# Two dense heads scored together on groups of the array's rows, and the remainder of an expert's tokens turned back by one transpose

## The reference

```python
a = rms_norm(h, attn_norm_g)
q_s, k_s, v_s, q_lat, kv_lat, k_rope = split(a @ w_in)
y_a = windowed_gqa(...)        # 8 heads of 64, 2 key heads, keys within 128 tokens and the meta tokens, ALiBi, sink
y_b = latent_attention(...)    # 8 dense heads: q = rms_norm(...) is 64 columns (nope) and 32 rotated (rope),
                               # k likewise with one rope part for all heads; every query sees all 1040 keys
h = h + concat(y_a, y_b) @ w_out
m = rms_norm(h, ffn_norm_g)
logits = m @ router_w + router_b          # 32 experts, each token goes to 4
y = swiglu(m_e @ w_gate[e], m_e @ w_up[e]) @ w_down[e] + b_down[e]      # of the tokens m_e of expert e
h = h + sum of y, weighted by the gate
```

## Time and profile before

| | |
|---|---|
| time, median of 3 runs | 2257.07 us (2256.37 to 2257.84) |
| the profiled execution | 2257.38 us, its span 2255.3 us |
| PE busy | 2211.1 us, 98% |
| weight loads (PEld) | 1743.8 us, 77% |
| DVE busy | 815.5 us, 36% |
| ACT busy | 485.9 us, 22% |
| POOL busy | 205.5 us, 9% |
| transfers | 490.37 MB, mean 217 GB/s |

### The profile page before, as it was taken

One profiled execution on the slowest core, in us unless ns is written; L12 is line 12 of the kernel. 1 busy time (PEld: TensorE's weight loads), 2 busy tenths in 40 slices (PEclk: granted clock), 3 DMA queues, 4 the chain that ended last, 5 costly groups with the idle time before them and its releaser, 6 DMA issues.

```text
span 2255.3 us, 37720 instructions
## 1 busy us (share of the span) xinstructions
PE 2211.1 (98%) x15544; PEld 1743.8 (77%) x15544; DVE 815.5 (36%) x2465; ACT 485.9 (22%) x1235; POOL 205.5 (9%) x229
## 2 busy tenths in 40 slices
PE   8998999999999899999999999999999999999998
PEld 4554666666666877887899999998788878878876
DVE  4555655555556322222222222222222222222222
ACT  3343544544445000000111111110000000001000
POOL 1000000000001111111111111010000000000000
PEclk9999999999999899999999999999999999999999
DMA  4000500000005897878878888899998998999881
GB/s 164 29 1 2 170 11 29 31 29 29 24 16 195 262 313 244 280 262 280 301 266 308 294 320 302 293 320 326 328 343 310 327 343 310 330 340 325 314 307 20
DMA packets 208573, 490.37 MB, mean 217 GB/s; under 512 B 22395, under 2 KB 23867, under 8 KB 208224
## 3 DMA queue, kind: packets, MB, share of 16 engines
q1 hardware_dynamic: 191824, 448.71, 55.1%
q0 software_dynamic: 14960, 39.07, 6.9%
q10 hardware_dynamic: 1616, 0.14, 0.1%
HBM read 463.49 MB, written 28.88 MB: 218 GB/s over the span
## 4 chain that ended last, share of the span: by engine, by line
PE 66%; issue 0%; DMA 0%; POOL 0%; POOLq 0%; ACT 0%; DVE 0%
PE gu_bank L2107 43%; PE ya_bank L2168 13%; PE ya_bank L2140 6%; PE yb_bank L2181 1%; PE xa_bank L2077 1%; PE xb_bank L2085 0%; PE yb_bank L2125 0%; PE xa_bank L2124 0%; PE ya_bank L2157 0%; DMA x_rows<-ffn_rows,first_tab 0%; POOLq L1669 0%; POOL out_y L1822 0%; ACT y_rows L1887 0%; DVE y_rows L1978 0%; PE yb_bank L2195 0%
## 5 line engine op out<-in xcount | busy, mean ns | idle before, releaser
L2107 PE MATMUL gu_bank<-xT,ring_head 128*128 128x128 f32 (+10 forms) x4160 | 507.5, 282 | 0.8 <-issue 0.8
L2107 PEld LDWEIGHTS gu_bank<-xT,ring_head 128*128 128x128 f32 x4160 | 498.7, 191 | 7.6 <-issue 7.3
L2107 PE MATMUL gu_bank<-xT,ring 128*128 128x128 f32 (+8 forms) x4032 | 484.8, 280 | 0.0
L2107 PEld LDWEIGHTS gu_bank<-xT,ring 128*128 128x128 f32 x4032 | 477.0, 191 | 3.8 <-issue 3.6
L1932 DVE TENSOR_SCALAR g_in<-gu_bank,bias_cur 128x128 f32<-128x128 f32 (+10 forms) x256 | 91.9, 359 | 644.7 <-PE gu_bank L2107 644.3
L1877 ACT ACTIVATE sig<-g_in 128x128 f32<-128x128 f32 (+10 forms) x256 | 80.9, 316 | 815.8 <-DVE g_in L1932 815.8
L2168 PE MATMUL ya_bank<-ring,hidden 128*128 128x512 f32 x480 | 208.9, 593 | 0.0
L2168 PEld LDWEIGHTS ya_bank<-ring,hidden 128*128 128x128 f32 x480 | 90.0, 190 | 107.8 <-issue 105.0
L556 PE MATMUL proj_bank<-w_in_sb,normT 128*128 128x512 f32 (+3 forms) x384 | 128.2, 487 | 0.0
L1285 PE MATMUL score_bank<-ring_head 96*128 96x512 f32 x256 | 126.9, 620 | 0.0
L1978 DVE TENSOR_TENSOR y_rows<-ya_bank,b_row 128x512 f32<-128x512 f32 x46 | 29.7, 687 | 268.7 <-PE ya_bank L2168 257.3
(11 more groups left out here) (348 smaller groups left out, 2285.4 us busy)
## 6 DMA issues: line engine op xcount, KB each, us to landing
ring<-in_w_down SPq DMA_DIRECT2D x42, 2048.0 KB, 12.2
ring_head<-in_w_up SPq DMA_DIRECT2D x33, 2048.0 KB, 8.9
ring_head<-in_w_gate SPq DMA_DIRECT2D x32, 2048.0 KB, 14.1
ring<-in_w_gate SPq DMA_DIRECT2D x32, 2048.0 KB, 14.6
ring<-in_w_up SPq DMA_DIRECT2D x31, 2048.0 KB, 9.1
ring_head<-in_w_down SPq DMA_DIRECT2D x22, 2048.0 KB, 11.9
b_row<-in_b_down SPq DMA_DIRECT2D x32, 512.0 KB, 9.2
xt<-in_x SPq DMA_DIRECT2D x8, 512.0 KB, 3.9
```

What stands on the lines that cost most here:

```text
L2107: last = nc.tensor.matmul(gu_bank[:, f % 2, i * 256:i * 256 + width], w[:, k, c * P:(c + 1) * P], xT[:, k, 0:width], start=(k == 0), stop= ...
```

## The change

In attend a step now has two heads or two local pairs: four dense steps and two local ones a tile (`UNITS` is 6). The keys and queries of the dense heads are stored as two arrays each: the nope parts of two heads on the two 64-row halves, and the rope parts of two heads, each twice, on four groups of 32 rows, one for each half of the keys. A dense step's scores are four rope matmuls of 32 rows (L1355 of the new kernel), one to each of the four banks of `score_bank`, and four nope matmuls of 64 rows (L1360) that add to them. The next scores wait until DVE has read all four banks (`max_ready`, `band_ready`).

DVE reads each bank once, by the operation that local heads had: it adds a column of zeros, keeps a running maximum and writes the scores to `probs` (in odd steps to `late_probs`, a part of the ring's fourth piece). ACT's exponential works in place there. The values of a step are done in two parts, with the transposes of inverse sums, normed rows and logits between them. The meta scores are eight matmuls of two heads each in four groups of output columns, and one transpose instead of two. The out projection takes the dense half of its inner dimension first and waits for the local half (`swa_mixed`) later. The first expert's fourth weight piece waits for the last transposes of `late_probs`.

In project, a tile has six transposes of keys instead of eight, by pairs of heads, and eight of queries as before; two more gain constants are fetched.

In experts, ACT copies the first 128 columns of a tall chunk to `yT` and the others to a tile `yT_more` with 16 columns a chunk, and one transpose (L2191) turns all eight chunks' rests. They come out as one part of 128 columns per partition, so the bias and the gate and slot tables are fetched by eight small transfers each, and the sum is added by parts of rows, as in the wider turns.

The diff, cut to the matmuls and transposes, DVE's passes and the tall turns:

```diff
-                    for hf in range(2):
-                        transposes(t, f"kT{hf}", [(i, k_raw[0:n, 4 * hf + i, :]) for i in range(4)])
+                    transposes(t, "kT0", [(i, k_nope[0:n, 2 * i:2 * i + 2, :].rearrange("p h c -> p (h c)"))
+                                          for i in range(4)])
+                    transposes(t, "kT1", [(i, k_rope[0:n, i].rearrange("p b s c -> p (b s c)")) for i in range(2)])
                     if t < MT:
                         pe.wait_ge(q_ready, tiles_to(s + 1))
-                        for hf in range(2):
-                            transposes(t, f"qT{hf}", [(i, q_raw[:, 4 * hf + i, :]) for i in range(4)])
+                        transposes(t, "qT0", [(i, q_nope[:, 2 * i:2 * i + 2, :].rearrange("p h c -> p (h c)"))
+                                              for i in range(4)])
+                        transposes(t, "qT1", [(i, q_rope[:, 2 * i:2 * i + 2].rearrange("p h a c -> p (h a c)"))
...
+                def dense_max(n, b, half):
+                    t, i = divmod(n, UNITS)
+                    h = 2 * i + b
+                    if b == 0:
+                        if half:
+                            dve.wait_ge(scores_done, n + 1)
+                        else:
+                            dve.wait_ge(half_done, n + 1)
+                            dve.wait_ge(meta_read, t + 1)
+                    link(v.tensor_tensor_reduce(
+                        out=probs_of(n)[:, b, half * 512:(half + 1) * 512], in0=score_bank[:, 2 * b + half, :], in1=zeros[:].to_broadcast([P, 512]),
+                        scale=1.0, scalar=half_max[:, b:b + 1] if half else meta_max[:, t % 2, h:h + 1],
+                        op0=ALU.add, op1=ALU.max, accum_out=all_max[:, b:b + 1] if half else half_max[:, b:b + 1]))
+                    if half:
+                        v.tensor_scalar(neg_max[:, n % 2, b:b + 1], all_max[:, b:b + 1], -1.0, None, ALU.mult)\
+                            .then_inc(max_ready, 1)
...
+                def wait_read(n):
+                    t, i = divmod(n, UNITS)
+                    if i < DENSE:
+                        pe.wait_ge(max_ready, t * MLA_HEADS + 2 * i + 2)
+                    else:
+                        pe.wait_ge(band_ready, t * SWA_HEADS + 4 * (i - DENSE) + 4)
 
                 def scores(n):
                     t, i = divmod(n, UNITS)
-                    j = at_fill["unit", n]
-                    bank = score_bank[:, j % 2, :]
-                    wait_fill_free(pe, j)
-                    if i < MLA_HEADS:
+                    if n:
+                        wait_read(n - 1)
+                    if i == OUT + 1 and t >= 1:
+                        pe.wait_ge(attn_added, t)
+                    if i < DENSE:
+                        m, s = divmod(i, 2)
+                        for g in range(4):
+                            b, half = g // 2, g % 2 ^ s
+                            r = slice(g * ROPE, (g + 1) * ROPE)
+                            nc.tensor.matmul(score_bank[:, 2 * b + half, :], q_roT[r, i, cols(t)], k_roT[r, m, half, :],
+                                             start=True, stop=False, skip_group_check=True)
                         for half in range(2):
-                            last = nc.tensor.matmul(bank[:, half * 512:(half + 1) * 512], mla_qT[:, i, cols(t)],
-                                                    mla_kT[:, i, half * 512:(half + 1) * 512], start=True, stop=True)
-                            if half == 0:
-                                last.then_inc(half_done, 1)
+                            for b in range(2):
+                                r = slice(b * NOPE, (b + 1) * NOPE)
+                                last = nc.tensor.matmul(score_bank[:, 2 * b + half, :], q_noT[r, i, cols(t)],
+                                                        k_noT[r, i, half * 512:(half + 1) * 512], start=False, stop=True,
+                                                        skip_group_check=True)
+                            last.then_inc(scores_done if half else half_done, 1)
                     else:
-                        for at, key, keys, _, _ in band_parts(t):
-                            for g in range(SWA_KV):
-                                r = slice(g * HD, (g + 1) * HD)
-                                last = nc.tensor.matmul(bank[:, g * 512 + at:g * 512 + at + keys],
-                                                        swa_qT[r, i - MLA_HEADS, cols(t)],
-                                                        swa_kT[r, key:key + keys], start=True, stop=True)
-                    last.then_inc(scores_done, 1)
-
...
+                def values(n, part):
                     t, i = divmod(n, UNITS)
-                    pair = i // 2
-                    if half == 0:
-                        pe.wait_ge(dve_T_out, n + 1)
-                        pe.wait_ge(act_T_out, at_act["unit", n] + 1)
-                        if pair == 0 and t >= 1:
-                            pe.wait_ge(mla_mixed, t)
-                    for k in range(4 * half, 4 * half + 4):
-                        for j in range(2):
-                            last = nc.tensor.matmul(mla_bank[j * VD:(j + 1) * VD, pair * P:(pair + 1) * P],
-                                                    mla_v[:, k, 2 * pair + j, :], probsT[:, (n - 1 + j) % 4, k, :],
-                                                    start=(pair == 0 and k == 0), stop=False, skip_group_check=True)
-                    if half:
+                    if i < DENSE:
+                        if part == 0:
+                            pe.wait_ge(dve_T_out, 2 * n + 2)
+                            pe.wait_ge(act_T_out, at_act["unit", 2 * n + 1] + 1)
+                            if i == 0 and t >= 1:
+                                pe.wait_ge(mla_mixed, t)
+                        for k in range(4 * part, 4 * part + 4):
+                            for x in range(2):
+                                last = nc.tensor.matmul(mla_bank[x * VD:(x + 1) * VD, i * P:(i + 1) * P],
+                                                        mla_v[:, k, 2 * i + x, :], probsT[:, (2 * n + x) % 4, k, :],
+                                                        start=(i == 0 and k == 0), stop=False, skip_group_check=True)
...
                 def turn_back(at, c):
 
-                    n, h = WIDTHS[at] - P, c // 4
+                    h = c // 4
                     cols = slice(c % 4 * P, (c % 4 + 1) * P)
                     pe.wait_ge(yt_out, talls(at) * DC + c + 1)
                     if c == 0:
                         pe.wait_ge(x_out, 2 * (at + 2))
-                        pe.wait_ge(biased_b, wides(at))
-                    if c == 4:
-                        pe.wait_ge(yb_half, talls(at) + 1)
-                    nc.tensor.transpose(xa_bank[:, h, cols], yT[:, c, 0:P], ident[:])
-                    last = nc.tensor.transpose(yb_bank[0:n, cols], yT[:, c, P:P + n], ident[:])
+                    last = nc.tensor.transpose(xa_bank[:, h, cols], yT[:, c, 0:P], ident[:])
                     if c % 4 == 3:
                         last.then_inc(ya_done if h else yr_half, 1)
+                    if c == DC - 1:
+                        pe.wait_ge(biased_b, wides(at))
+                        nc.tensor.transpose(yb_bank[:, 0:P], yT_more[:].rearrange("p c q -> p (c q)"), ident[:]).then_inc(yb_done, 1)
...
                 def results(b, at, i):
                     if tall(at):
+                        if talls(at) == 0:
+                            act.wait_ge(yt_zero, 1)
                         for c in range(DC):
                             act.wait_ge(yt_done, talls(at) * DC + c + 1)
-                            nc.scalar.copy(yT[:, c, 0:WIDTHS[at]], ya_bank[:, c % 2, 0:WIDTHS[at]]).then_inc(yt_out, 1)
+                            nc.scalar.copy(yT[:, c, :], ya_bank[:, c % 2, 0:P])
+                            nc.scalar.copy(yT_more[:, c, 0:WIDTHS[at] - P], ya_bank[:, c % 2, P:WIDTHS[at]])\
+                                .then_inc(yt_out, 1)
```

743 lines of the change are left out of this document (386 added, 357 removed).

## The result

The changed kernel took 2234.52 us (median of 4 runs, 2234.02 to 2235.06) and the kernel before, run beside it, 2257.45: a ratio of 0.9894, 95% interval 0.9883 to 0.9906. That is 22.9 us less; forecast were 33, so the time is 10.5 us above the forecast 2224 and inside the range. The profiled execution took 2234.02 us, its span is 2232.3.

What follows compares the result with a forecast made beforehand. PE's instructions were taken to bound attention and experts. From 2257.4 us, attention -26.2, experts -6.9 and project 0 gave 2224.3, so 2224 us, with a range from 2208 to 2248.

Steps and rivals of the forecast that it cites:

- One sign that was named for being wrong: Attention on PE: idle time ahead of the scores would show the prediction wrong; no size given.
- Dense steps, -24.6: Attention: packed scores make a dense step 6.85 us, 0.77 less than the pair before, times 32: -24.6 us.
- cuts of the values, +7.2: Attention: whole-array transposes between the halves of a step's values cost 0.25 us more each, some 29 places: +7.2 us.
- Local steps, -6.4: Attention: two local units joined into a step go from 6.38 to about 5.98 us; 16 steps, -6.4 us.
- entering and leaving costs about 0.3: Local scores on PE: switching into and out of split array use costs about 0.3 us, saved once per joined step.
- I cost the wait at nothing: Dense steps: PE's wait for DVE to read the score banks costs nothing, with about 0.6 us left.
- Nothing, and at most some us if the queues share badly: First expert's fourth weight piece, now waiting for the last transposes: not late, so no cost, at most some us.
- The experts' -6.9: Experts: one transpose per turn for the chunks' remainders, 63 fewer at 0.11 us each on PE: -6.9 us.
- the price of two rope matmuls at a time: Dense scores, rival: only two rope matmuls run together, 0.86 x 32 = 27.5 us more, 2251.5 us; chance 0.10.
- DVE's slack of "about 0.6": Dense step: DVE's chain ends at 6.2 us, PE reaches the next scores at 6.85, leaving about 0.6 us.
- the switches that the pairs save 0.15: Dense step: 0.1 us off where value parts follow without a switch, 0.05 where the last transposes run into scores.

Runs made afterwards that it cites:

- the experiment with the rows ahead: Changed kernel with the seventh tile's normed rows sent out before the first expert's third and fourth weight pieces instead of behind them: 2234.34 us, ratio 0.9893.
- the experiment with more passes: Changed kernel with the last of DVE's four passes of each dense step done three times: 2262.59 us, ratio 1.0020.

## Why the prediction was right, and where its sizes were off

The mechanism held at most of its steps: rope runs four-fold, the scores take 2.99 us, the pass 0.75, DVE's chain ends at 6.2 us, PE is busy for 60.15 of 60.55 us in a full tile, 63 transposes are gone. One sign that was named for being wrong did come: idle time ahead of the scores behind DVE, 2.63 us, though in the first tile only. The direction and the range were right. The sizes fell short by 10 us, and these are the terms:

- *Dense steps, -24.6, and cuts of the values, +7.2.* Right in the sum. By the distances between PE's starts in a full tile, scores, transposes and values of the dense heads went from 30.8 to 28.7 us; the forecast is 4 x 0.77 less and 0.9 more for the cuts, -2.2 as well. In part that is luck: the scores gave 2.7 us a tile, forecast 2.4, and the transposes and values took 0.5 more, forecast 0.3. A cut costs 0.22, forecast 0.25.
- *Local steps, -6.4.* Failed: in the same way of counting they went from 12.9 to 12.5 us a tile, 0.4 less where the forecast has 0.8. The step is "entering and leaving costs about 0.3": it was read from the 16 records of a local unit and took the records of 16 columns for almost free. In the trace of after the loads of their weights start 0.11 us apart (428.38, 428.49, 428.60, 428.71), whether the records have 128 columns or 16. Two units together take 1.90 us, 16 waves of 0.11 and 0.14 for entering, so joining them saves 0.1 a step in the scores and not 0.3; nor did the values get cheaper (1.17 and 1.18 a half, 2.34 together). At 0.4 a tile that is some 3 us, half of the 6.0 that attention is short of.
- *"I cost the wait at nothing".* Failed: the chain of DVE was worked out for one dense step, and there it fits, but not for the first tile, the normed rows and the last tile. PE waits 7.1 us for DVE in attention, and 0.7 for ACT. The trace of before has 3.8 us of waits for ACT and DVE in the same stretch, beside the 1.52 ahead of the out projection, so some 4 us are new. With the local steps that is a little more than attention is short of; the clock at its start, low for longer in the profile of before, goes the other way.
- *"Nothing, and at most some us if the queues share badly".* Failed: +1.5. I looked at whether the fourth weight piece comes late, not at what else stands behind the weights on SP's queue. 8 MB of weights start when the last scores are done, the rest of the tile has become shorter, and the rows of the seventh tile, issued at 695.16, landed at 710.0, after 14.8 us; the store a tile earlier, issued at 651.13, took 2.6. The experiment with the rows ahead shows it.
- *The end.* In no term: +2.3, with the tall turns' new transfers. I priced these as issues that hide beside PE; POOL's closing wait has nothing beside it.

The experts' -6.9 came as -6.5. Of the rivals, the price of two rope matmuls at a time is confirmed (27.5, measured 27.0 in the tiles). DVE's slack of "about 0.6" is not one number: the experiment with more passes gives 1.1 and 0.4 us at two places, and at the normed rows there is none. What the forecast had wrong in the account is who brings the gain: I gave the scores 0.61 us a step and the switches that the pairs save 0.15; measured are 0.22 a step for the packing, net, and 1.54 a tile for all the rest of the change, 0.60 of it idle time that no term had.

## What to carry to other kernels

Price a packed matmul by the stream it saves less the switches around it and less what PE then waits for because it arrives earlier, and count the switches of the whole step in the order it will have: here the packing by itself was worth 0.89 of 2.43 us a tile. Work out a wait for the first and the last round of a loop too, not only for one in the middle. When a stage becomes shorter, look at every transfer that its end triggers and at what is queued behind these. Of an edit that adds transfers on an engine, ask also what it adds where that engine closes the kernel.

## What the runs showed that was not expected

- Four 32-row groups: 8 records of 512 columns in 1.07 us, 1.92 with two groups used twice. In the local scores a record of 16 columns costs as much as one of 128, 0.11 us.
- From packed use back to whole-array use and values, some 0.14 us are lost a step, and 0.40 a tile in a wait for DVE that the packing uncovers.
- POOL's closing wait was 7.4, 9.4 and 8.0 us with 201, 266 and 356 transfers issued.
- The first tile, to its sixth step, took from 37.3 to 41.2 us in kernels with the same instructions there: 37.3 where the granted clock stood at the lower level for 3.4 us, 39.4 where it did for some 14, 41.2 where it fell twice. Full tiles agreed within 0.01 us.
